# The token mixer of a two-layer decoder step, rebuilt: decay levels by products, sample states in a buffer of their own and decayed on VectorE

## The reference, cut to what matters

```
z = rmsnorm(x) @ w_in;  q, f, i, g, xr, gr = split(z)           # six groups of 512 columns
forget = lb + (1 - lb)*sigmoid(f);  k = (1 - lb)*sigmoid(-f);  q = silu(q)
S[t] = forget[t] * S[t-1] + k[t] v[t]^T;  o[t] = q[t] S[t]      # 4 heads, 128 x 128 state each
o = rmsnorm_per_head(o) * hg_norm * silu(g)
xc = causal_conv4(xr);  a = exp(-8 softplus(-lambda) * sigmoid(xc W_ra))
h[t] = a h[t-1] + sqrt(1 - a^2) * sigmoid(xc W_ix) * xc;  r = h * gelu(gr)
x = x + concat(o, r) @ w_out
```

## Time and profile before

| | |
|---|---|
| Median of 3 runs | 1715.77 us (1711.54 to 1716.29) |
| Profiled execution, span of its core | 1714.0 us |
| Mean granted TensorE clock | 0.955 |
| Mixer of layer 1, first projection matmul to last output tile | 28.1 to 210.4 us |
| Mixer of layer 2, the same | 430.8 to 608.1 us |
| Dense SwiGLU between | 218.9 to about 422 us |
| Experts and end | from 615 us |

### The profile page before, as it was taken

How to read it: one execution, slowest core, us unless ns; L and a number is a source line. 1 busy time by engine, 2 the same in 40 slices (tenths; PEclk the granted TensorE clock), 3 DMA queues, 4 the chain that set the end, 5 groups by cost and what they waited for, 6 DMA issues and landing times.

```text
span 1714.0 us, 24614 instructions
## 1 busy us (share of the span) xinstructions
PE 1604.6 (94%) x8844; PEld 1376.9 (80%) x8844; DVE 1358.8 (79%) x1264; ACT 1011.9 (59%) x840; POOL 160.5 (9%) x130
## 2 busy tenths in 40 slices
PE   6895889999996798999999999999999999999997
PEld 5895789998896687887888888888888788788885
DVE  5997665666697748888888888888888888888985
ACT  4644343334545326767766776776676777677672
POOL 2245400000144510000000000000000000000000
PEclk8996899999997679999999999999999999999999
DMA  8451245545343017998998998998998998998990
GB/s 260 130 160 61 92 151 182 171 164 179 124 142 105 25 57 266 368 355 291 375 359 275 370 370 281 373 355 293 362 364 288 357 368 295 360 361 299 352 341 26
DMA packets 212918, 433.00 MB, mean 253 GB/s; under 512 B 7064, under 2 KB 62800, under 8 KB 212880
## 3 DMA queue, kind: packets, MB, share of 16 engines
q1 hardware_dynamic: 208176, 421.59, 69.9%
q0 software_dynamic: 1792, 5.42, 1.0%
q10 hardware_dynamic: 2912, 5.47, 0.9%
HBM read 426.57 MB, written 5.95 MB: 252 GB/s over the span
## 4 chain that ended last, share of the span: by engine, by line
PE 76%; DVE 14%; ACT 5%; issue 3%; DMA 1%; PEld 0%; POOL 0%; DVEq 0%; ACTq 0%; SPq 0%; PEldq 0%
PE ps L1338 22%; PE ps L1340 22%; PE ps L1339 22%; DVE w_lo L773 3%; PE ps L1607 3%; ACT w_hi L482 2%; PE ps L1654 1%; PE ps L1354 1%; DVE xc L927 1%; DVE lev L899 1%; DVE sc L915 1%; DMA out_dram<-hstate 1%; DVE lev L901 1%; DVE xc L1034 1%; DVE y_f L1245 1%
## 5 line engine op out<-in xcount | busy, mean ns | idle before, releaser
L773 DVE TENSOR_TENSOR w_lo<-raw,w_hi 128x2048 fp32r<-128x2048 f32 x401 | 921.7, 2311 | 188.7 <-ACT w_hi L482 181.7
L482 ACT ACTIVATE w_hi<-raw 128x2048 fp32r<-128x2048 f32 x401 | 763.5, 1917 | 332.9 <-PE ps L1340 208.7
L1338 PE MATMUL ps<-w_hi,xg 128*128 128x512 f32 x896 | 359.4, 401 | 7.4 <-DVE w_lo L773 7.4
L1340 PE MATMUL ps<-w_hi,xg 128*128 128x512 f32 x896 | 354.5, 396 | 0.0
L1339 PE MATMUL ps<-w_lo,xg 128*128 128x512 f32 x896 | 354.1, 395 | 0.0
L1338 PE MATMUL ps<-h_hi,w_hi 128*128 128x264 f32 x736 | 216.5, 294 | 23.5 <-DVE h_lo L800 15.5
L1339 PE MATMUL ps<-h_lo,w_hi 128*128 128x264 f32 x736 | 211.5, 287 | 0.0
L1340 PE MATMUL ps<-h_hi,w_lo 128*128 128x264 f32 x736 | 211.5, 287 | 0.0
L1338 PEld LDWEIGHTS ps<-w_hi,xg 128*128 128x128 f32 x896 | 169.0, 189 | 52.5 <-DVE w_lo L773 16.7
L1340 PEld LDWEIGHTS ps<-w_hi,xg 128*128 128x128 f32 x896 | 168.8, 188 | 40.1
L1339 PEld LDWEIGHTS ps<-w_lo,xg 128*128 128x128 f32 x896 | 169.2, 189 | 36.1
(11 more groups left out here) (282 smaller groups left out, 1831.1 us busy)
## 6 DMA issues: line engine op xcount, KB each, us to landing
raw<-in_moe_w_dram SPq DMA_DIRECT2D x336, 1024.0 KB, 6.2
raw<-in_ffn_w_dram SPq DMA_DIRECT2D x33, 1024.0 KB, 5.5
raw<-in_w_in_dram SPq DMA_DIRECT2D x24, 1024.0 KB, 5.5
raw<-in_w_out_dram SPq DMA_DIRECT2D x8, 1024.0 KB, 4.9
out_dram<-hstate POOLq DMA_DIRECT2D x2, 2048.0 KB, 10.5
x_rows<-in_x_prompt_dram SPq DMA_DIRECT2D x1, 1024.0 KB
out_dram<-y_rows ACTq DMA_DIRECT2D x2, 512.0 KB
out_dram<-s_fin POOLq DMA_DIRECT2D x2, 256.0 KB, 9.8
```

Of the source, the lines that this page charges most:

```text
L482: act.activation(w_hi[:, s, :], raw[:, r, :], ACT.Copy).then_inc(hi_made, 1)
L773: dve.tensor_tensor(w_lo[:, s, :], raw[:, r, :], w_hi[:, s, :].bitcast(F32), ALU.subtract).then_inc(split, 1)
L1338: pe.matmul(out, l_hi, r_hi, start=start, stop=False)
L1340: return pe.matmul(out, l_lo, r_hi, start=False, stop=stop)
```

## The change

`cum`, the log, GpSimd's subtractions and ScalarE's exponentials go. The key and the query are kept as products with the decay up to the border of their block, and each level extends them in place. All GpSimd elementwise work goes: its queue has DMAs alone. ScalarE applies silu and gelu directly. The order of the input groups is now f, q, xr, g, i, gr; three PSUM banks rotate for the tiles and three for scores. Levels start with unit 5 of 12 instead of 7, the convolution one unit earlier relative to its data, and the gates come between units 8 to 11. TensorE no longer waits for itself: the split slots are released by `z_done` and `y_done` directly (`freed`).

The core of the diff, in this order: GpSimd's queue, VectorE's `extend` and `new_state`, TensorE's `spread_value`, its projection loop, its output tiles, and the end of the dense SwiGLU's `down`:

```diff
-                for k in range(8):
-                    pool.tensor_tensor(xv[:, :, :, 0, :], mid, cv[:, :, :, 0, :], ALU.subtract
-                    pool.tensor_tensor(xv[:, :, :, 1, :], cv[:, :, :, 1, :], mid, ALU.subtract
...
-                    pool.tensor_tensor(st, st, f_b, ALU.mult).then_inc(st_decayed, 1)
...
+                if l:
+                    pool.wait_ge(st_stored, 16 * l)
+                pool.dma_start(hstate[:, :, :], state_hgrn[l].rearrange("b h k v -> k (b h) v")
+                               ).then_inc(st_landed, 16)
...
+                def extend(k):
+                    half = 1 << k
+                    kv, qv, fv = parts(key), parts(qd), parts(forget)
+                    even, odd = fv[:, :, :, 0, half - 1:half], fv[:, :, :, 1, half - 1:half]
+                    dve.wait_ge(sc_done, SCORES * l + 2 * k + 4)
+                    dve.tensor_tensor(kv[:, :, :, 0, :], kv[:, :, :, 0, :], odd.broadcast_to(wide),
+                                      ALU.mult).then_inc(lev_ready, 1)
+                    dve.tensor_tensor(qv[:, :, :, 1, :], qv[:, :, :, 1, :], even.broadcast_to(wide),
+                                      ALU.mult).then_inc(lev_ready, 1)
+                    link(dve.tensor_tensor(odd, odd, even, ALU.mult))
...
                 def new_state(b):
                     dve.wait_ge(kv_done, NSAMPLE * l + b + 1)
-                    dve.wait_ge(st_decayed, NSAMPLE * l + b + 1)
+                    every = hstate[:, HEADS * b:HEADS * (b + 1), :]
+                    link(dve.tensor_tensor(every, every, bc(f_s[:, :, b:b + 1], P), ALU.mult))
...
-                    for part in range(2):
-                        ins = pe.matmul(ps[:, 5 + b % 3, :], ones_r[:, :],
-                                        v_diag[b % 2][:, part, :, :].rearrange("p h v -> p (h v)"),
+                    for h in range(HEADS):
+                        ins = pe.matmul(ps[:, 5 + b % 3, P * h:P * h + P],
+                                        v_s[:, h, b:b + 1].broadcast_to([P, P]), ident[:, :],
...
-                    pe.wait_ge(z_done, 24 * l + t + 1)
-                    pe.sem_inc(used, 1)
+                    if u == 4:
+                        pe.wait_ge(qf_ready, l + 1)
+                        scores(0, zq, 0)
+                        scores(1, zq, 1)
+                    if u >= 4:
+                        level(u - 4)
...
+                    if u >= GATE_LAG and u < GATE_LAG + HEADS:
+                        gate_pair(u - GATE_LAG)
...
+                for c in range(4):
+                    pe.wait_ge(split, ob + c // 2 + 1)
+                    out_part(c, MERGE_ORDER[:HEADS], True, False)
...
+                for c in range(DC):
+                    if c < 4:
+                        out_part(c, MERGE_ORDER[HEADS:], False, True).then_inc(y_done, 1)
+                    else:
+                        out_part(c, MERGE_ORDER, True, True).then_inc(y_done, 1)
+                    spread_value(c)
...
-                pe.wait_ge(y_done, s * DC + 2 * DC)
-                pe.sem_inc(used, 1)
```

More of the change, by code:

```diff
@@ L605, in mixer @@
-                for n in range(3, 8):
-                    gate(n)
+                    if u == GATE_LAG + HEADS + 2:
+                        v_out(0)
+                        v_out(1)
+                    if GATE_LAG + SPLIT <= u < GATE_LAG + SPLIT + HEADS:
+                        gate_pair(u - GATE_LAG - SPLIT)
                 act.wait_ge(gates_ready, 8 * (l + 1))
                 for j in range(HEADS):
-                    act.activation(zx[:, j, :], lev[1][:, j, :], ACT.Tanh,
+                    act.activation(zx[:, j, :], zf[:, j, :], ACT.Tanh,
@@ L1356, in norm, with project @@
                 ins.then_inc(ssq_done, 1)
-            def project(base, j, bank, x_hi=h_hi, x_lo=h_lo, order=range(DC), parts=None):
+            def project(base, j, bank, parts=None):
                 _, s, _, _ = unit_of(base)
@@ L1380, in scores @@
+                def scores(n, right, c, across=False, half=0):
+                    bank = product(n)
                     for h in range(HEADS):
                         rc = 1 if across else c
-                        ins = pe.matmul(ps[:, 4 + n % 4, P * h:P * h + P],
-                                        left[:, h, P * c:P * c + P],
-                                        right[:, h, P * rc:P * rc + P], start=True, stop=True)
+                        s, t = P * c, P * rc
+                        ins = pe.matmul(ps[0:P - half, bank, P * h + half:P * h + P],
+                                        key[:, h, s:s + P - half], right[:, h, t + half:t + P],
+                                        start=True, stop=True)
@@ L1385, in scores @@
                     ins.then_inc(sc_done, 1)
[L1386 removed]
                 def level(k):
[L1389 to L1392 removed]
+                    if k:
+                        pe.wait_ge(lev_ready, 14 * l + 2 * k)
+                    for c in range(2 if k < 7 else 1):
+                        scores(2 * k + 2 + c if k < 7 else 18, qd, c, across=(k == 7),
+                               half=64 if k == 6 else 0)
@@ new lines, in gate_pair @@
+                def gate_pair(j):
+                    pe.wait_ge(conv_ready, HEADS * l + j + 1)
+                    if j == 0 and l == 0:
+                        pe.wait_ge(gw_landed, 16 * 8)
+                    for kind in range(2):
+                        if j:
+                            pe.wait_ge(gates_ready, 8 * l + 2 * j + kind - 1)
+                        pe.matmul(ps[:, GATE_BANK[kind], 0:T], gate_w[:, l, kind, j, :],
+                                  xc[:, j, :], start=True, stop=True).then_inc(gates_done, 1)
@@ L1395, in mixer, with turn @@
+                def turn(n, src, c, done):
+                    bank = product(n)
+                    for h in range(HEADS):
+                        ins = pe.transpose(ps[:, bank, P * h:P * h + P],
+                                           src[:, h, P * c:P * c + P], ident[:, :])
+                    ins.then_inc(done, 1)
                 for u in range(IN_UNITS):
@@ L1470, in mixer @@
                 pe.sem_inc(o_done, 1)
+                pe.wait_ge(kd_tok_ready, 2 * (l + 1))
+                for h in range(HEADS):
+                    for c in range(2):
+                        ins = pe.matmul(ps[:, 7, P * h:P * h + P], k_tok[:, c, h, :],
+                                        v_tok[:, c, h, :], start=(c == 0), stop=(c == 1))
+                ins.then_inc(fin_done, 1)
                 def spread_value(b):
-                    pe.wait_ge(diag_ready, 2 * (NSAMPLE * l + b + 1))
                     if b < 3:
```

682 lines of the change are left out of this document (292 added, 390 removed).

## The result

The changed kernel takes **1636.41 us** (median of 4 runs, 1634.04 to 1638.53) beside 1713.65 us of the kernel before on the same chip: ratio 0.9547, 95% interval 0.953 to 0.9563. The forecast was 1661.0 with a range of 1645 to 1686. Sign and places were right; the gain, 82.0 us between the two profiled spans (1714.0 and 1632.0), is half as large again as the 54.3 forecast for the span. By the medians 77.2 us were gained: the profiled execution of the changed kernel is the fastest of its four (1634.04 us), so some 5 of the 82.0, and of the table by parts, are chance of the execution.

The account below looks back on a forecast made before the run. The prediction took TensorE's chain of waits (76%) and its standstills in the mixers as the bound. Terms of -27.5 - 29.6 - 2.5 + 0.9 - 0.6 + 2.6 = -56.7, less 2.4 hand-overs, gave 1661 us, range 1645 to 1686.

Parts of the forecast that it names:

- 11 x 0.30, goes in part: Dense SwiGLU: the down steps' share of TensorE's waits for itself partly disappears, -2.5 us, between 0 and -3.3.
- the state reads behind them keep their 11.9: Mixer, behind the prompt products: the state reads take 11.9 us as before, ending 111.1 us after the start.
- 28.4 and 26.3 with hand-overs: Gains forecast for the mixers of layers 1 and 2: 29.6 and 27.5 us, with 1.2 of hand-overs taken off each.
- 84.0: Mixer projection: time in us from the start to the end of unit 11, with levels, gate pairs and sample product.
- 14.3 was forecast: Behind the state reads: final state 4.0, head sums 3.4, first halves of tiles 5.9, about 1 for head norm and merges.
- The rival of the low clock (8%): Output tiles' first halves all run at half clock after the state reads, 10.6 for 5.9 us; total 1673; chance 8%.
- The 1.2 of hand-overs: Each layer: some 12 uncounted hand-overs of 0.1 us, giving back 2.4 us of the gain in all.
- The forecast's 2.9 for the rates: Layer 1's mixer: VectorE makes the rates ahead of the queries, about half covered, so first scores come some 2.9 us late.
- The 2.6 loss at layer 2's end: Behind layer 2's last tile: later store delays VectorE's clears, ending at 17.1 where logits were taken at 14.5; 2.6 us lost.
- The +0.9 of the last spread and the -0.6 of the store: Next norm: the last spread_value ahead of its sums costs 0.9 us per layer; layer 1's no longer awaiting the store saves 0.6.
- the rival at 10%: End of the projection: VectorE late for another reason, the 12.35 us wait per layer before the last level stays; 1686; chance 10%.
- The load of the states did not delay layer 1 (8%): Rival, layer 1's first units: the 2 MB state load delays weight units by up to 6 us; total 1667; chance 8%.

Follow-up runs that it names:

- e1: Changed kernel with TensorE's wait for its own last matmul put back at the end of each of the 11 SwiGLU down steps: 1643.9 us.
- e9: Changed kernel with the self-wait in each SwiGLU down step put back and a semaphore increment from TensorE's queue behind it: 1645.4 us.
- e8: Changed kernel with state reads of 120 columns each in place of one, samples in reverse order: 1629.5 us.
- e4: Changed kernel with TensorE held up before the last level of each layer while six small transfers run one after the other: 1664.2 us.
- e10: Changed kernel without TensorE's self-wait behind the reads, a gate pair moved between the values' transposes, the last spread ahead of the last tile: 1630.9 us.
- e11: Changed kernel with the changes of e8 and e10 together: 1627.7 us.
- e2: Changed kernel with TensorE's wait for itself put back at the end of each of the 12 projection units of a layer: 1645.3 us.
- e3: Changed kernel with GpSimd computing 16 unused products of 512 columns beside the levels in each layer: 1660.8 us.

## Why the prediction was wrong, and where it was right

Of the 27.7 us that the sum for the span missed (82.0 against 54.3), 17.6 lie in the two mixers, 6.6 in the SwiGLU with its norms, 2.2 at the start, 2.3 ahead of the experts and -1.0 in them. The mechanisms of the change were right; two steps of pricing failed. One is the SwiGLU's "11 x 0.30, goes in part". The other, the larger, is "the state reads behind them keep their 11.9", with what follows them at half clock.

**The SwiGLU's -2.5 (0 to -3.3) measured -8.6.** The first step prices the self-wait with the idle time of the table of waits, and counts down's share of it "in part". e1 and e9 give 6.6 for the wait and 1.5 for the increment in the queue. The trace of before had it: 1.05 from start to start against 0.12 between neighbours. In the mixers the prediction priced a unit from start to start (5.8), and there the unit came out, at 5.8 to 6.1.

**The mixers, 28.4 and 26.3 with hand-overs, measured 37.5 and 34.8.** In layer 2 the large terms were mis-sized on the same side:
- Unit 11 ended 82.2 behind the start, not 84.0. A level was priced 2.02, the length of its row; from start to start it costs 1.78, seven times. (A gate pair costs 0.70 and not 0.95, the units behind one 6.0 and not 5.8, which cancel.)
- The state reads "keep their 11.9": 9.66 here, 8.83 in layer 1, 8.8 to 11.6 in the runs with one-column reads. This term is no constant; it depends on when in the reads the clock falls: 2.0 us behind their start in layer 2 of the kernel before, 4.3 here. Even the forecast's lower end, 8.1 at full clock, was too long: e8 needs 7.30.
- From the reads to the second halves 14.3 was forecast, 12.0 measured. The rival of the low clock (8%) feared that the first halves of the output tiles would run at half; TensorE did not stop behind the reads, the granted clock was back at 1.00 by 494, and the head sums ran partly, the tiles wholly at it. Final state (3.54 from start to start, 4.0 forecast), head sums (2.2, 3.4) and the wait of 1 us for the merges, which did not occur, make the 2.3.
- The 1.2 of hand-overs in each layer was not seen; overlapping rows more than pay for them. Between unit 11 and the reads 14.7 passed for 15.2, behind the first halves 24.0 for 24.4.

In layer 1 the reads and what follows them up to the second halves took 20.0 where 26.2 was forecast (21.6 in layer 2): 6.2 of the 9.1. Part of that is luck, since the clock fell late there. The forecast's 2.9 for the rates came out near its size for another reason. TensorE waited 0.06 for the first scores, so the rates were covered; but 2.10 were lost one and a half units in, where ScalarE's first copies out of PSUM came late, behind two table loads of 1.28 each and a wait of 2.28 for VectorE's setup steps. The first scores came 3.6 later than in layer 2.

That idle time ahead of the reads made them slow was my own first explanation, and e4 refutes it.

**Small terms.** The 2.6 loss at layer 2's end came where it was forecast, and was given back by chance. The clears ended 17.2 us behind the last tile (17.1 forecast), and VectorE took the logits right behind them, at 17.25, where it had taken them at 14.5. In size that is the forecast, by its mechanism about 1.0: the logits themselves ended only 16.2 behind the last tile, TensorE being at half clock longer than before. Where the last spread stands ahead of the last tile (e10, e11), the logits are taken at 14.3 and 14.4. The stretch as a whole grew by 0.3 alone because from the taking of the logits to the first matmul that gathers tokens (L1607 before, L1556 after) 7.5 us passed instead of 10.0, with TensorE back at full clock for a few us (columns as in rows 2; the clock ahead of the DMA share):

```profile
626.00:628.00 2.00, 1.87 (x10) 1.78 (x9) 1.63 (x4) 1.85 (x2) 0.00 (x0) 0.50 0.00 0
545.00:547.00 2.00, 1.27 (x12) 1.28 (x12) 1.83 (x7) 1.59 (x2) 0.00 (x0) 0.98 0.00 0
```

(The kernel before, then the changed kernel.) In e2, e3 and e9, with the logits taken at the same 17.3 and the clock at 0.50 from there on, the stretch lasts 41.6 or 41.7 us and not 39.1. The +0.9 of the last spread and the -0.6 of the store cancel within 0.15 (norm 8.5 before, 8.64 after). The 2.2 at the start are at least partly chance: the runs with the same start reach the first projection matmul at 25.5 to 27.5 us.

**Right.** TensorE sets the pace in the projection, and VectorE keeps up at 0.69 for a broadcast product, 2.29 for a split, 0.69 for a scan. The wait before the last level is gone (the rival at 10% fails). The load of the states did not delay layer 1 (8%), though the rival's mechanism is there: the load lands 13.3 us after its issue, and beside it the second and third weight units land 15.4 and 17.8 us after theirs (9.2 and 11.6 before). They are there at 25.2 and 28.3 us, and ScalarE copies them from 29.5 on, behind the norm, without a wait. The wide decays are hidden, on VectorE, GpSimd or ScalarE. The experts differ by 1.0 us of 1067.

What stays open: why the clock falls 2 us into the reads in one execution and 5 in another, and with it how much of the mixers' gain another execution would keep. The runs show that it falls in each of them with one column, and not with 120.

## What to carry to other kernels

Price a step on TensorE by the distance from start to start in the trace: the length of a row holds a tail that the next instruction overlaps, and the idle column leaves out the overlap that a wait destroys. A wait of TensorE for its own last matmul, with a semaphore instruction behind it, cost 0.5 to 1.0 us each time here; let the engine that needs the buffer wait for that matmul instead. And look for stretches in which TensorE is busy at half clock: here 64 one-column matmuls ran faster with 120 columns each.

## What the runs showed of the hardware

A busy TensorE without idle time lost its full clock: in the reads of one column it went from 1.00 to 0.50 in every trace (eleven runs, both layers), and with 120 columns, in reverse order, it stayed at 1.00 (three runs). A semaphore increment in TensorE's own queue behind a wait cost about 0.16 us on the path (18.16 for 18.00 us a step, e9 and e1). Between VectorE and GpSimd the one that began first kept its time, and the other paid (a split at 2.29 us when it began first, 3.04 when GpSimd had). And six transfers in a row, each waiting for the one before, held TensorE up by 11.66 us at a price of 13.7 on the path: the clock behind the gap cost 2.0, not more.
